# Output projection: four pairs of blocks in seven products for eight, with x loaded as it is used

## The chip, the cores and the metric

The kernel runs on all 8 cores of one Trainium2 chip. Each core computes one sequence of the batch (2048 tokens). The metric is the device time in microseconds of the slowest core. The kernel before and the kernel after are timed on the same chip.

## The reference, cut to what matters

One layer of a streaming encoder, with D = 2048 channels and 2048 tokens per sequence:

```python
h = rmsnorm(x, norm1_w) * (1.0 + sc1) + sh1
merged = sigmoid(ma) * (y_a @ w_up_a) + sigmoid(mb) * (y_b @ w_up_b)   # of h @ w_in and two recurrences
x = x + gt1 * (merged @ w_o)                    # w_o: 2048 x 2048, the output projection
h = rmsnorm(x, norm2_w) * (1.0 + sc2) + sh2
x = x + gt2 * swiglu(h, w_ffn_in, w_ffn_out)
return rmsnorm(x, final_norm_w)
```

The modulation values (sh1, sc1, gt1, sh2, sc2, gt2) come from c @ w_ada, per sequence.

## The kernel before

**Order of the work.** Tokens are taken in two stages (`s` = 0 and 1, 1024 tokens each, two halves of 512). Activations lie channel by channel: a tile `mg[k]` is 128 channels x 1024 tokens in bf16, and `H(t, hf)` is one half of it. A stage runs through the input projections and recurrences (heads), the merge, the output projection with the norm behind it, and the FFN in four quarters. Between is one long list of operations: `Graph.op` records each with the tiles it reads and writes, a cost and a key (the running sum of TensorE time `g.K` plus an offset), and `Graph.schedule` lays them out by a list scheduler from these costs. Each engine then runs its operations in the order so fixed; `emit` puts the waits in. All instructions of a kind are recorded by helpers, so they bear the helpers' lines: L478 `dense_half`, L488 `product`, L530 `plain`, L621 `norm_finish`, L799 `vgroup` (TensorE); L388 `act` (ScalarE); L392 `tt`, L412 `stt`, L495 `vtt` (VectorE); L429 every `dma`.

**Plain blocks.** A block of 128 output channels is `dense_half` for each half: 16 matmuls of 128x128 weights by 512 columns into one PSUM bank. `proj(fc, hfs, w)` does so for w_o: `stt` adds gt1 times the bank to the residual `xres[fc]` (f32), ScalarE squares the result, and VectorE adds the squares into `accD`. Blocks 0 to 9 do both halves in turn, blocks 10 to 15 first the one half of all six, then `h2half(0)` (the norm and 16 tiles of the next input), then the other half and `h2half(1)`.

**Seven for eight.** `winograd` computes a pair of output blocks as a 2 x 2 block product: the four quadrants of the weight pair (a11, a12, a21, a22, each 8 blocks of 128x128) by the even and odd input tiles and the two token halves. It takes four sums of weights on VectorE (`tt16`, 1024 columns of bf16), 7 products of 8 matmuls in place of 8, two copies out of PSUM on ScalarE, and three additions on VectorE; four results come out, two in PSUM banks and two in SBUF. The right sides (differences of the input tiles, 512 columns of bf16) are made once for all pairs by `make` in `right_sides`. It gives three new sets of 8 tiles (`t2`, `t3`, `t4`) and overwrites the second half of the even inputs by the fourth (`t1`). The merge's gates use it for blocks 2 to 15 (`w_m`), the FFN's input from its fourth block on (`w_fi`), and a variant for the FFN's output (`w_fp`). The output projection does not: it is plain throughout.

**Weights.** All weights lie in HBM as f32 and are cast by DMAs that GpSimd (POOL) issues. `wload` puts one block (1 MB read, 512 KB written) into the next of six slots of 4 KB per partition, `wload2` a pair (twice that) into the next two. A load waits until the last reader of its slots is done, and POOL issues in the order of the schedule. In stage 0 the merge also loads two w_ada chunks per block through these slots, for `ada_chunk` (one `stt` over 2048 columns with an accumulator, on VectorE). Blocks 10 and 11 of w_o have tiles of their own (`wextra`). The chunks of w_ada are worked off in stage 0: the last 14 of them 4 in the output projection (blocks 6 to 9) and 10 in the FFN's first quarter, there through one buffer at 192 KB.

**x.** The residual is loaded once more for the update: `xload(fc)` puts 512 KB into `xres[fc]` from SP. All 16 are recorded ahead of the projection; each waits for the space, which is that of the merge's right sides and `up` weights (blocks 0 to 7) and of `yT` (8 to 15), and blocks 6 and 7 in addition for `mops`, results of the merge.

Of the kernel before, what the change touches and what calls it, by code (L numbers as in the profile page):

```python
# [17 lines left out]
KB = 1024  # L18
# [225 lines left out]
def build_nc(trace=None):  # L244
    nc = bass.Bass("TRN2", target_bir_lowering=False)

    def din(name, shape):
        return nc.dram_tensor(name, list(shape), F32, kind="ExternalInput").ap()
# [13 lines left out]
    w_upb_d = din("w_upb_l", [16, 128, 1024])  # L262
    w_o_d = din("w_o_l", [16, 128, 2048])
    w_fi_d = din("w_fi_l", [44, 128, 4096])
# [4 lines left out]
    with ExitStack() as es:  # L269
# [267 lines left out]

        def right_sides(acts, t2, t3, t4):

            ev, od = acts[0::2], acts[1::2]  # L540
            hk = len(ev)
            bs = {'11': [H(t, 0) for t in ev], '21': [H(t, 0) for t in od], '22': [H(t, 1) for t in od],
                  't1': [H(t, 1) for t in ev], 't2': t2, 't3': t3, 't4': t4}

# [3 lines left out]
            def make():  # L548
                for i in range(hk):
                    sub(t3[i], bs['22'][i], bs['t1'][i])  # L550
                    sub(t2[i], t3[i], bs['11'][i], ALU.add)
                    sub(t4[i], bs['21'][i], t2[i])
                for i in range(hk):
                    sub(bs['t1'][i], bs['t1'][i], bs['11'][i])

# [415 lines left out]
        def ada_some(n, own=None):  # L971
            for _ in range(n):
                if ada_todo:
                    m = ada_todo.pop(0)
                    if own:
                        ada_chunk(m, wpair(own, w_ada_d[m - 32], psem[7]), 0.0)
                    else:
                        ada_chunk(m, wload(w_ada_d[m - 32], 2048, lag=5.0, slot=5 if nslot[0] == 5 else None), 0.0)
# [12 lines left out]
        for s in range(NST):  # L991
# [98 lines left out]

            dring[:] = [0, 1, 2, 3]
            accD = sb(HT, 1024, F32)
            rsD = sb(190 * KB, 1024, F32)
            d_q = ring(HT + 8 * KB, 3, 512, F32)
            d_t = ring(182 * KB, 4, 512, F32)

            def xload(fc):
                dma('sp', xres[fc], xT[fc, :, tok0:tok0 + ST], xsem[fc], writes=[xres[fc]], nbytes=1 << 19, key=-40,
                    after=[mops[4 + fc]] if 5 < fc < 8 else ())

            def proj(fc, hfs, w):
                def ev(hf, p):
                    x = H(xres[fc], hf)
                    stt(x, p, col(gt1h, fc), x, ALU.mult, ALU.add)
                    q = d_q() if fc else H(accD, hf)
                    act(q, x, AF.Square)
                    if fc:
                        tt(H(accD, hf), H(accD, hf), q, ALU.add)
                for hf in hfs:
                    dense_half(w, mg, hf, ev)  # L1110

            def h2half(hf):
                norm_finish(accD, rsD, hf)
                for fc in range(16):
                    t_ = d_t()
                    tt(t_, H(xres[fc], hf), H(rsD, hf), ALU.mult)
                    act(H(mg[fc], hf), t_, AF.Identity, bias=col(mod, 48 + fc), scale=col(a2, fc))
            for fc in range(16):
                xload(fc)
            for fc in range(10):  # L1120
                proj(fc, (0, 1), wload(w_o_d[fc], 2048))
                if s == 0 and 5 < fc:
                    ada_some(1)

            def wextra(i, src):
                t = sb(HT + (24 + 4 * i) * KB, 2048, BF16)
                dma('pool', t, src, psem[6 + i], writes=[t], nbytes=1 << 20, key=-20.0)
                return t
            ws = [wextra(i, w_o_d[10 + i]) for i in range(2)] + [wload(w_o_d[fc], 2048) for fc in range(12, 16)]
            for hf in range(2):  # L1130
# [112 lines left out]
            for q in range(4):  # L1243
# [8 lines left out]
                for j in range(nj):  # L1252
# [11 lines left out]
                    if s == 0 and q == 0:  # L1264
                        ada_some(2 if 0 < j < 6 else 0, sb(192 * KB, 2048, BF16))
                    if s + 1 < NST and q > 0:
# [73 lines left out]
def prep_inputs(x, c, w_ada, b_ada, norm1_w, w_in, w_gk2, b_gk2, lb_param, a_norm_w, b_norm_w,  # L1340
# [23 lines left out]
        "w_upb_l": _colchunks(f(w_up_b)[0]),  # L1364
        "w_o_l": _colchunks(f(w_o)[0]),
        "w_fi_l": _blockpairs(f(w_ffn_in)[0]),
# [41 lines left out]
```

## Time and profile before

| | us |
|---|---|
| median of 3 timed runs | 3780.18 |
| lowest, highest | 3710.52, 3817.74 |
| profiled execution, its own time | 3529.29 |
| its span on core 3, the slowest | 3528.2 |
| TensorE busy in it | 3423.4 |
| VectorE busy | 2155.5 |
| ScalarE busy | 1085.0 |

The profile is of one execution and of its slowest core, core 3. Its span runs from the first to the last instruction; its own time is 1.1 us longer. PE is TensorE, PEld its weight loads, DVE VectorE, ACT ScalarE, POOL GpSimd, SP the engine that issues the plain loads. The two output projections lie at about 882 to 1000 us (stage 0) and 2565 to 2676 us (stage 1). Times within the profile are us from its start.

### The profile page before, as it was taken

What the parts mean: (1) busy time and instruction counts of PE and PEld (TensorE: products, weight loads), DVE (VectorE), ACT (ScalarE), POOL (GpSimd) and SP (SyncE); (2) the same over time, 40 slices, a digit from 0 to 9 for tenths busy, and PEclk for the clock granted to TensorE, in tenths of its full rate; (3) what the DMA queues carried; (4) which work ended last, traced back from release to release, by engine and by line L of the source; (5) the groups of instructions that cost most, each with busy time, mean ns of one, the idle gap of its engine ahead of it and who ended that gap; (6) DMA issues with size and microseconds to landing.
All of it is one profiled execution on the core that took longest, in us unless ns stands there. A gap on an engine that the chain in (4) does not pass through costs nothing.

```text
span 3528.2 us, 48466 instructions; the slowest of 8 cores (3509.2 to 3528.2 us)
## 1 busy us (share of the span) xinstructions
PE 3423.4 (97%) x17336; PEld 1590.3 (45%) x17336; DVE 2155.5 (61%) x3769; ACT 1085.0 (31%) x1668; POOL 319.6 (9%) x564
## 2 busy tenths in 40 slices
PE   5899999999999999999999999999999999999997
PEld 2444444444444444444444444444444444444445
DVE  2277777776477866757586564544446575665747
ACT  3256445111142122121366553311114102111016
POOL 1111010111000000000010000000100000000004
PEclk8899999999999999999999999999999999999998
DMA  9966555888847575655595343354563445454552
GB/s 193 158 108 104 91 92 91 138 142 156 173 80 128 106 120 100 119 81 101 97 204 123 67 70 68 67 93 87 99 152 62 89 79 95 78 99 81 95 96 97
DMA packets 108047, 377.43 MB, mean 107 GB/s; under 512 B 11297, under 2 KB 28705, under 8 KB 92449
## 3 DMA queue, kind: packets, MB, share of 16 engines
q0 software_dynamic: 75888, 314.97, 52.9%
q1 hardware_dynamic: 31922, 59.36, 5.8%
q8 instruction: 142, 2.33, 0.3%
q14 instruction: 95, 0.78, 0.1%
HBM read 672.44 MB, written 16.78 MB: 195 GB/s over the span
## 4 chain that ended last, share of the span: by engine, by line
PE 89%; DMA 7%; DVE 2%; issue 1%; SPq 1%; ACT 0%; DVEq 0%; POOL 0%; ACTq 0%; POOLq 0%
PE PS L488 48%; PE PS L478 27%; PE PS L799 6%; PE PS L530 4%; DMA SB<-w_ada_c 1%; DMA SB<-xT 1%; DVE SB L392 1%; PE PS L682 1%; DMA SB<-w_fp_l 1%; DMA SB<-w_in_l 1%; DMA SB<-w_o_l 1%; SPq L429 1%; DMA SB<-w_m_l 1%; DMA SB<-w_fi_l 1%; PE PS L921 0%
## 5 line engine op out<-in xcount | busy, mean ns | idle before, releaser
L488 PE MATMUL PS<-SB 128*128 128x512 bf16 x8176 | 1772.4, 379 | 4.6 <-DVE SB L392 2.8
L488 PEld LDWEIGHTS PS<-SB 128*128 128x128 bf16 x8176 | 799.0, 98 | 972.9 <-issue 17.6
L478 PE MATMUL PS<-SB 128*128 128x512 bf16 (+2 forms) x5052 | 1075.9, 371 | 35.6 <-DVE SB L412 21.0
L478 PEld LDWEIGHTS PS<-SB 128*128 128x128 bf16 x5052 | 484.4, 99 | 584.8 <-issue 53.8
L388 ACT ACTIVATE SB<-SB 128x512 f32<-128x512 f32 (+5 forms) x790 | 462.9, 623 | 824.7 <-DVE SB L392 541.8
L495 DVE TENSOR_TENSOR SB<-SB 128x1024 bf16<-128x1024 bf16 (+2 forms) x1000 | 536.9, 563 | 240.3 <-PE PS L488 161.1
L392 DVE TENSOR_TENSOR SB<-PS,SB 128x512 f32<-128x512 f32 (+2 forms) x536 | 359.7, 673 | 374.1 <-PE PS L488 257.5
L388 ACT ACTIVATE SB<-PS 128x512 f32<-128x512 f32 (+2 forms) x546 | 328.7, 614 | 677.5 <-PE PS L488 371.4
L412 DVE SCALAR_TENSOR_TENSOR SB<-PS,SB 128x512 f32<-128x512 f32 (+2 forms) x528 | 365.6, 712 | 254.1 <-PE PS L478 106.1
L392 DVE TENSOR_TENSOR SB<-SB 128x512 f32<-128x512 f32 (+6 forms) x639 | 377.6, 611 | 152.3 <-ACT SB L388 120.4
L388 ACT ACTIVATE PS<-PS 128x512 f32<-128x512 f32 x158 | 92.0, 582 | 793.1 <-PE PS L488 754.8
L412 DVE SCALAR_TENSOR_TENSOR SB<-SB,PS 128x128 f32<-128x128 f32 (+3 forms) x452 | 208.8, 463 | 168.5 <-PE PS L478 135.2
L388 ACT ACT_TABLE_LOAD x158 | 202.7, 1283 | 125.1 <-PE PS L478 62.4
L799 PE MATMUL PS<-SB 128*128 128x512 bf16 x1024 | 230.1, 379 | 1.0 <-DMA SB<-w_v_l 1.0
L412 DVE SCALAR_TENSOR_TENSOR SB<-SB 128x2048 bf16<-128x2048 bf16 (+2 forms) x160 | 212.8, 1349 | 7.2 <-ACT SB L388 5.4
L799 PEld LDWEIGHTS PS<-SB 128*128 128x128 bf16 x1024 | 98.0, 98 | 114.8 <-issue 2.0
L530 PE MATMUL PS<-SB 128*128 128x512 bf16 x640 | 141.6, 379 | 0.0
L429 POOL DMA_DIRECT2D SB<-w_fi_l x88 | 46.4, 528 | 944.7 <-PE PS L488 784.1
L530 PEld LDWEIGHTS PS<-SB 128*128 128x128 bf16 x640 | 62.5, 98 | 74.1 <-issue 1.1
L429 POOL DMA_DIRECT2D SB<-w_in_l x100 | 52.9, 532 | 451.3 <-PE PS L478 210.3
L420 DVE CAST SB<-PS 128x512 bf16<-128x512 f32 x68 | 46.7, 689 | 63.2 <-PE PS L799 61.2
L429 POOL DMA_DIRECT2D SB<-w_fp_l x48 | 25.3, 528 | 473.0 <-PE PS L488 473.0
(55 smaller groups left out, 862.3 us busy)
## 6 DMA issues: line engine op xcount, KB each, us to landing
SB<-w_fi_l POOLq DMA_DIRECT2D x88, 1024.0 KB, 8.6
SB<-w_fp_l POOLq DMA_DIRECT2D x48, 768.0 KB, 6.9
SB<-w_in_l POOLq DMA_DIRECT2D x70, 512.0 KB, 6.9
SB<-xT SPq DMA_DIRECT2D x64, 512.0 KB, 22.9
SB<-w_ada_l POOLq DMA_DIRECT2D x64, 512.0 KB, 7.1
SB<-w_m_l POOLq DMA_DIRECT2D x32, 1024.0 KB, 9.0
SB<-w_ada_c POOLq DMA_DIRECT2D x32, 512.0 KB, 22.3
SB<-w_v_l POOLq DMA_DIRECT2D x32, 512.0 KB, 6.2
```

Of the source, the lines that this page charges most:

```text
L388: return g.op('act', lambda e: e.activation(out=out.ap, in_=in_.ap, func=func, **kw), reads=[in_] + aps, writes=[out], cost=cost, key=key, ...
L392: return g.op('dve', lambda e: e.tensor_tensor(out=outap if outap is not None else out.ap, in0=in0ap if in0ap is not None else in0.ap, in1 ...
L412: return g.op('dve', lambda e: e.scalar_tensor_tensor(out=out.ap, in0=in0.ap, scalar=v, in1=in1.ap, op0=op0, op1=op1, **kw), reads=[in0, i ...
L420: g.op('dve', lambda e: e.tensor_copy(out=outap if outap is not None else out.ap, in_=inap if inap is not None else in_.ap), reads=[in_], ...
L429: return g.op(q, lambda e: e.dma_start(out=oa, in_=ia), reads=list(reads), writes=list(writes), dsem=sem, nbytes=nbytes, cost=0.6, key=key ...
L478: fns = [(lambda e, k=k: e.matmul(p.ap, w.ap[:, k * 128:(k + 1) * 128], H(acts[k], hf).ap, start=(k == 0), stop=(k == nk - 1))) for k in ks]
L488: fns = [(lambda e, k=k: e.matmul(p.ap, w.ap[:, k * 128:(k + 1) * 128], acts[k].ap, start=(first and k == 0), stop=(k == nk - 1), skip_gro ...
L495: g.op('dve', lambda e: e.tensor_tensor(out=out, in0=in0, in1=in1, op=op), reads=reads, writes=writes, cost=0.16 + n * 0.00052, key=key)
L530: mm([(lambda e, k=k: e.matmul(p.ap, wk[k].ap, H(acts[k], hf).ap, start=(k == 0), stop=(k == nk - 1))) for k in range(k0, k0 + GK)], wk[k0 ...
L682: mm([lambda e, p=p, k=k, hf=hf: e.matmul(p.ap, w.ap[:, (k - k0) * 128:(k - k0 + 1) * 128], H(hT[k], hf).ap, start=(k == k0), stop=(k == k ...
L799: fns = [(lambda e, i=i, j=j, p=p, tb=tb: e.matmul(p.ap, hT[4 * i + j].ap[:, tb * 128:(tb + 1) * 128], ws[i].ap[:, j * 512:(j + 1) * 512], ...
```

## The change

Blocks 2 to 9 become four pairs through `winograd`; blocks 0, 1 and 10 to 15 stay plain. The right sides of `mg` are made in four new sets of tiles, so that `mg` itself stays as it is for the plain blocks behind (`t1` is given). They are recorded behind block 1 with a key 8 us ahead. Sets `o_1` and `o_2` lie where the last tiles of `hT` were, `o_3` and `o_4` where the merge's results were kept. The projection's PSUM ring has six banks in place of four. x is loaded for blocks 0 to 5 ahead; every further `xload` is recorded behind a block or pair and waits (`after`) for the last x update recorded before it. The extra w_o tiles move to 202 KB and to the start of `hT`. The four w_ada chunks of the projection go to the FFN's first quarter, which takes 14, alternating between two buffers.

```diff
@@ -260,7 +260,8 @@
     w_v_d = din("w_v_l", [16, 128, 2048])
     w_upa_d = din("w_upa_l", [16, 128, 1024])
     w_upb_d = din("w_upb_l", [16, 128, 1024])
-    w_o_d = din("w_o_l", [16, 128, 2048])
+    w_o_d = din("w_o_l", [8, 128, 2048])
+    w_op_d = din("w_op_l", [4, 128, 4096])
     w_fi_d = din("w_fi_l", [44, 128, 4096])
     w_fp_d = din("w_fp_l", [3, 8, 128, 3072])
     w_fo_d = din("w_fo_l", [16, 128, 1024])
@@ -535,23 +536,30 @@
         def rr(t, c):
             return t.ap.rearrange("p (n t) -> p n t", t=c)
 
-        def right_sides(acts, t2, t3, t4):
+        def right_sides(acts, t2, t3, t4, t1=None):
 
             ev, od = acts[0::2], acts[1::2]
             hk = len(ev)
             bs = {'11': [H(t, 0) for t in ev], '21': [H(t, 0) for t in od], '22': [H(t, 1) for t in od],
-                  't1': [H(t, 1) for t in ev], 't2': t2, 't3': t3, 't4': t4}
+                  't1': t1 or [H(t, 1) for t in ev], 't2': t2, 't3': t3, 't4': t4}
+            b12 = [H(t, 1) for t in ev]
 
             def sub(out, x, y, op=ALU.subtract):
                 vtt(out.ap, x.ap, y.ap, op, [x, y], [out], 512, key=-8.0)
 
             def make():
-                for i in range(hk):
-                    sub(t3[i], bs['22'][i], bs['t1'][i])
+                for i in range(hk if t1 else 0):
+                    sub(t1[i], b12[i], bs['11'][i])
+                    sub(t2[i], bs['22'][i], t1[i])
+                for i in range(hk if t1 else 0):
+                    sub(t3[i], t2[i], bs['11'][i])
+                    sub(t4[i], bs['21'][i], t2[i])
+                for i in range(0 if t1 else hk):
+                    sub(t3[i], bs['22'][i], b12[i])
                     sub(t2[i], t3[i], bs['11'][i], ALU.add)
                     sub(t4[i], bs['21'][i], t2[i])
-                for i in range(hk):
-                    sub(bs['t1'][i], bs['t1'][i], bs['11'][i])
+                for i in range(0 if t1 else hk):
+                    sub(b12[i], b12[i], bs['11'][i])
 
             def again():
                 for i in range(hk):
@@ -973,7 +981,7 @@
                 if ada_todo:
                     m = ada_todo.pop(0)
                     if own:
-                        ada_chunk(m, wpair(own, w_ada_d[m - 32], psem[7]), 0.0)
+                        ada_chunk(m, wpair(own[m % 2], w_ada_d[m - 32], psem[6 + m % 2]), 0.0)
                     else:
                         ada_chunk(m, wload(w_ada_d[m - 32], 2048, lag=5.0, slot=5 if nslot[0] == 5 else None), 0.0)
                     blk = m // 16
@@ -1088,24 +1096,47 @@
                 merge_b(fc)
 
 
-            dring[:] = [0, 1, 2, 3]
+            dring[:] = [0, 1, 2, 3, 4, 5]
+            dpos[0] = 0
+            spos[0] = 2
             accD = sb(HT, 1024, F32)
             rsD = sb(190 * KB, 1024, F32)
             d_q = ring(HT + 8 * KB, 3, 512, F32)
             d_t = ring(182 * KB, 4, 512, F32)
 
+            r_so = ring(194 * KB, 4, 1024, BF16)
+            o_tt = [sb(o_ * KB, 512, F32) for o_ in (188, 190, 192, 74)]
+            o_n = [0]
+
+            def r_to():
+                o_n[0] += 1
+                return o_tt[o_n[0] % 4]
+            o_1, o_2, o_3, o_4 = [[sb(o_ + KB * i, 512, BF16) for i in range(8)]
+                                  for o_ in (HT + 14 * KB, HT + 22 * KB, 172 * KB, 180 * KB)]
+            o_rights, o_sums, _ = right_sides(mg, o_2, o_3, o_4, o_1)
+            lastx = [None]
+
             def xload(fc):
                 dma('sp', xres[fc], xT[fc, :, tok0:tok0 + ST], xsem[fc], writes=[xres[fc]], nbytes=1 << 19, key=-40,
-                    after=[mops[4 + fc]] if 5 < fc < 8 else ())
+                    after=[lastx[0]] if lastx[0] else ())
+
+            def add_x(fc, hf, p):
+                x = H(xres[fc], hf)
+                lastx[0] = stt(x, p, col(gt1h, fc), x, ALU.mult, ALU.add)
+                q = d_q() if fc else H(accD, hf)
+                act(q, x, AF.Square)
+                if fc:
+                    tt(H(accD, hf), H(accD, hf), q, ALU.add)
+
+            def proj2(i, wp):
+                def evac(c11, c12, c21, c22):
+                    for n_, c_ in enumerate((c11, c12, c22, c21)):
+                        add_x(2 + 2 * i + n_ // 2, (0, 1, 1, 0)[n_], c_)
+                winograd(wp, 8, o_rights, r_so, r_to, evac)
 
             def proj(fc, hfs, w):
                 def ev(hf, p):
-                    x = H(xres[fc], hf)
-                    stt(x, p, col(gt1h, fc), x, ALU.mult, ALU.add)
-                    q = d_q() if fc else H(accD, hf)
-                    act(q, x, AF.Square)
-                    if fc:
-                        tt(H(accD, hf), H(accD, hf), q, ALU.add)
+                    add_x(fc, hf, p)
                 for hf in hfs:
                     dense_half(w, mg, hf, ev)
 
@@ -1115,18 +1146,22 @@
                     t_ = d_t()
                     tt(t_, H(xres[fc], hf), H(rsD, hf), ALU.mult)
                     act(H(mg[fc], hf), t_, AF.Identity, bias=col(mod, 48 + fc), scale=col(a2, fc))
-            for fc in range(16):
+            for fc in range(6):
                 xload(fc)
-            for fc in range(10):
+            for fc in range(2):
                 proj(fc, (0, 1), wload(w_o_d[fc], 2048))
-                if s == 0 and 5 < fc:
-                    ada_some(1)
+                xload(6 + fc)
+            o_sums()
+            for i in range(4):
+                proj2(i, wload2(w_op_d[i]))
+                xload(8 + 2 * i)
+                xload(9 + 2 * i)
 
             def wextra(i, src):
-                t = sb(HT + (24 + 4 * i) * KB, 2048, BF16)
+                t = sb((202 * KB, HT + 4 * KB)[i], 2048, BF16)
                 dma('pool', t, src, psem[6 + i], writes=[t], nbytes=1 << 20, key=-20.0)
                 return t
-            ws = [wextra(i, w_o_d[10 + i]) for i in range(2)] + [wload(w_o_d[fc], 2048) for fc in range(12, 16)]
+            ws = [wextra(i, w_o_d[2 + i]) for i in range(2)] + [wload(w_o_d[fc], 2048) for fc in range(4, 8)]
             for hf in range(2):
                 for i in range(6):
                     proj(10 + i, (hf,), ws[i])
@@ -1262,7 +1297,7 @@
                     elif q > 0 or j > 2:
                         hidden2(j, wload2(w_fi_d[hc]))
                     if s == 0 and q == 0:
-                        ada_some(2 if 0 < j < 6 else 0, sb(192 * KB, 2048, BF16))
+                        ada_some(2 if 0 < j < 8 else 0, [sb(188 * KB, 2048, BF16), sb(192 * KB, 2048, BF16)])
                     if s + 1 < NST and q > 0:
                         for _ in range(3 if q == 2 else 2):
                             if nexta[0] < 64:
@@ -1362,7 +1397,8 @@
         "w_v_l": w_v,
         "w_upa_l": _colchunks(f(w_up_a)[0]),
         "w_upb_l": _colchunks(f(w_up_b)[0]),
-        "w_o_l": _colchunks(f(w_o)[0]),
+        "w_o_l": _colchunks(np.concatenate([f(w_o)[0][:, :256], f(w_o)[0][:, 1280:]], axis=1)),
+        "w_op_l": _blockpairs(f(w_o)[0][:, 256:1280].reshape(2048, 4, 2, 128).transpose(0, 2, 1, 3).reshape(2048, 1024)),
         "w_fi_l": _blockpairs(f(w_ffn_in)[0]),
         "w_fp_l": np.stack([_blockpairs(w_fo[q * 1536:q * 1536 + 1536]) for q in range(3)]),
         "w_fo_l": _colchunks(w_fo_last),
```

## Rows read from the trace of the kernel before

**Rows 1.** The profile page: span and cores; busy us of each engine, share of the span.
```profile
span 3528.2 us, 48466 instructions; the slowest of 8 cores (3509.2 to 3528.2 us)
...
PE 3423.4 (97%) x17336; PEld 1590.3 (45%) x17336; DVE 2155.5 (61%) x3769; ACT 1085.0 (31%) x1668; POOL 319.6 (9%) x564
```

**Rows 2.** Windows: us; busy of PE, PEld, DVE, ACT, POOL; clock, DMA share, GB/s.
```profile
614.00:863.00 249.00, 248.15 (x1149) 112.39 (x1150) 178.09 (x269) 47.38 (x80) 34.31 (x66) 1.00 0.84 142
2561.00:2630.00 69.00, 69.00 (x321) 31.24 (x320) 28.94 (x41) 11.33 (x18) 4.22 (x8) 1.00 0.73 169
1020.00:1130.00 110.00, 110.00 (x511) 49.86 (x510) 81.56 (x133) 22.80 (x37) 9.35 (x18) 1.00 0.73 120
1130.00:1200.00 70.00, 69.81 (x324) 31.53 (x323) 53.02 (x99) 11.79 (x25) 3.76 (x8) 1.00 0.58 107
```

**Rows 3.** Waits of TensorE (total, times, longest): whole span of core 3; core 5.
```profile
PE PS L478 <- DVE SB L412: 21.0, 9, 5.0
...
PE PS L478 <- DMA SB<-w_o_l: 4.6, 1, 4.6
...
PE PS L478 <- DMA SB<-w_o_l: 5.7, 1, 5.7
```

**Rows 4.** The chain of waits around both projections: start, us, what.
```profile
872.12 28.13 DMA SB<-w_o_l
...
2554.43 102.74 PE PS L478 x476
```

**Rows 5.** The timeline at the first projection (start, us, engine), and w_ada's loads.
```profile
863.02 37.69 SPq L429 DMA_DIRECT2D SB<-xT  x16
...
871.42 24.34 PE L478 MATMUL PS<-SB 128*128 128x512 bf16 x112
...
1019.85 0.53 POOL L429 DMA_DIRECT2D SB<-w_ada_l  x1 [18.42 <-DVE SB L495]
...
1131.02 0.53 POOL L429 DMA_DIRECT2D SB<-w_ada_l  x1 [2.56 <-DVE SB L412]
```

**Rows 6.** Windows of TensorE behind the stall: us, PE busy, clock, DMA share.
```profile
900.00:904.00 4.00, 3.61 (x9) 0.50 1.02 235
904.00:908.00 4.00, 4.00 (x14) 0.72 1.01 252
```

**Rows 7.** Groups by shape, 882 to 980 and 2425 to 2554: busy, mean ns.
```profile
L412 DVE SCALAR_TENSOR_TENSOR SB<-PS,SB 128x512 f32<-128x512 f32 x26 | 19.5, 750 | 39.1 <-PE PS L478 39.1
L392 DVE TENSOR_TENSOR SB<-SB 128x512 f32<-128x512 f32 x23 | 15.9, 691 | 13.9 <-ACT SB L388 13.9
L412 DVE SCALAR_TENSOR_TENSOR SB<-SB 128x2048 bf16<-128x2048 bf16 x4 | 9.1, 2284 | 0.0
...
L495 DVE TENSOR_TENSOR SB<-SB 128x1024 bf16<-128x1024 bf16 x22 | 15.1, 687 | 12.3 <-PE PS L488 11.8
L388 ACT ACTIVATE SB<-PS 128x512 f32<-128x512 f32 x20 | 11.9, 597 | 15.7 <-PE PS L488 15.7
```

**Rows 8.** The timeline of VectorE behind the first projection: the FFN's right sides.
```profile
1009.03 8.74 DVE L392 TENSOR_TENSOR SB<-SB 128x512 f32<-128x512 f32 x14
...
1019.23 3.44 DVE L495 TENSOR_TENSOR SB<-SB 128x512 bf16<-128x512 bf16 x10
...
1029.76 2.09 DVE L495 TENSOR_TENSOR SB<-SB 128x512 bf16<-128x512 bf16 x6
```

**Rows 9.** DMA queues, packets, MB and share, 863 to 900.3.
```profile
q0 software_dynamic: 1032, 3.60, 58.7%
q1 hardware_dynamic: 1089, 4.00, 41.9%
```

**Rows 10.** Landing times: all w_fi loads; the one issued at 1029.51; all xT.
```profile
SB<-w_fi_l POOLq DMA_DIRECT2D x88, 1024.0 KB, 8.6
...
SB<-w_fi_l POOLq DMA_DIRECT2D x1, 1024.0 KB, 8.3
...
DMA to landing us min/median/max: 2.2/7.5/42.2
```

## Prediction before the result

> **What bounds the kernel now.** I read the busy shares and the cores' spans first, then windows by stage, then the chain of waits, and last the transfers around the one stall found. TensorE is busy 97% of the span [rows 1]: whoever adds nothing to TensorE and takes no wait from it changes nothing. The cores lie within 0.6% of each other (3509.2 to 3528.2 us) [rows 1], so core 3, the slowest, stands for all. The kernel passes the output projection twice, once in each half of the tokens. Around the second pass TensorE is never idle (69 us busy of 69 in the stretch read), while VectorE is busy 42% of it [rows 2]. Around the first pass it is idle once: a wait of 4.6 us for w_o on core 3, and of 5.7 us on core 5, where it is longest [rows 3]. Other waits of TensorE lie outside the projection.
>
> The stall's story is in the chain and the timeline [rows 4, 5]. The weights of block 2 take the first half of the slot pair that w_m of block 15 held, whose last quarter (a22) is read by the last product; so that load is issued at 872.12, as the last of the loads that the end of the merge sets free, and lands 28.13 us later. SP has meanwhile put all 16 loads of x into the same 16 DMA engines, from 863.02 on. Blocks 0 and 1 run 112 matmuls with the merge's tail, until 895.76; the weights come at 900.25. Behind the wait the granted clock is 0.50 for 4 us and 0.72 for the next 4, so the engine first runs at 1.2 GHz, then at 2.4 again [rows 6]: (1 - 0.50) x 3.6 busy us + (1 - 0.72) x 4 = 2.9 us more. The stall costs 4.6 + 2.9 = 7.5 us.
>
> **Part 1, products.** In each pass blocks 2 to 9 take 8 x 2 x 16 = 256 matmuls now and 4 x 7 x 8 = 224 afterwards; 64 fewer in both passes. In the long chain piece 476 matmuls take 102.74 us, 0.216 each [rows 4], so 64 x 0.216 = 13.8 us. Nothing hides TensorE, so all of it is gained if nobody makes it wait.
>
> **Part 2, what VectorE gets per pair.** Four left-side sums over 1024 columns, three f32 additions, four updates of x and four additions of squares. By their durations [rows 7]: 4 x 0.69 + 3 x 0.69 + 4 x 0.75 + 4 x 0.69 = 10.6 us, within 56 x 0.216 = 12.1 us of TensorE. That is an upper bound, since back to back they overlap: 14 f32 additions take 8.74 us, 0.62 each [rows 8], which makes about 9.6 us, 80%. In the first pass's merge VectorE is busy 72% and in the FFN output stage 76%, while TensorE misses 0.85 us of 249 and 0.2 of 70 [rows 2]. ScalarE has two copies and four squares per pair, 0.60 each, under 4 us [rows 7]. I take 0.5 us in all for small waits, the merge's share of 0.85 in 249 on the pairs' 97 us and a little more. The bounds are 0 (TensorE has no wait there that could go) and 5 us, the longest wait for an x update's or merge's stt in the whole trace [rows 3], once.
>
> **Part 3, the right sides.** 32 bf16 differences of 512 columns come to stand between the last read of hT and the first pair. Ten such take 3.44 us [rows 8], so 32 take 11.0 us. In the second pass hT is free at 2554.4, 48 matmuls of the merge and 64 of blocks 0 and 1 follow, 24.2 us; the product with t3 comes 4 products (6.9 us) later, the one with t4 6 products (10.4 us): the last group is due at +34.6 us. By then VectorE owes ten operations of the merge (6.9), the sums (11.0), blocks 0 and 1 (4 x 0.75 + 2 x 0.69 = 4.4), the left sides of two pairs (5.5) and two additions (1.4): 29.2 of 34.6 us. t1 and t2 come first in the order and are due at +25.9 to +27.7: 6.9 + 5.5 + 2.8 + 4.4 = 19.6. It fits, and costs 0. The upper bound goes by a sum twice as wide at its full duration, 0.69 [rows 7]: 22 us in place of 11, 40.3 of 34.6, 5.7 us late in each pass. Below 0 nothing is to be had, as TensorE has no wait there.
>
> **Part 4, loads.** In the first pass the pair's 1 MB load (w_op 0) takes both halves of w_m 15's slots, so it also cannot be issued before 872.12, behind w_op 1 and the two extra w_o tiles: six half-MB units in total, as now. What falls away is x: only blocks 0 to 5 are loaded ahead. Up to 900.3 the weights' queue moved 3.60 MB, the x queue 4.00 MB in 41.9% of 37.3 us [rows 9], 3.9 us per MB; six x loads are 3.15 MB, 0.85 MB fewer, 3.3 us earlier: w_op 0 lands at about 897.0. The first product is due at 895.76, so I forecast a wait of 1.2 us, and a second of some 0.8 for the first left side behind it: 2 us, too short to expect the slow clock. Of the 7.5 us, 5.5 come back. Bounds: all 7.5 if the queue drains quicker; nothing if the 1 MB load, twice as long as what it replaces, lands at 900.25 again. In the second pass no such conflict exists: that slot pair is free a whole merge block earlier, as no w_ada load takes slots there.
>
> The paced x loads come when the last update before them is done: blocks 8 and 9 behind the first pair, needed 36 us later; blocks 14 and 15 behind the fourth, needed by block 14 after 5 x 3.45 = 17 us. One x load lands after 7.5 us in the median, counting the bursts [rows 10]. SP has nothing behind them but later x loads and stores. So no cost.
>
> Four w_ada chunks per kernel go from the first projection to the FFN's first quarter, which takes 14 instead of 10, with two buffers. One costs 2.28 us of VectorE and a small addition, 2.4 [rows 7]. Today's ten are issued from 1019.85 to 1131.02 [rows 5], so nine at most run in the stretch 1020 to 1130, where VectorE is busy 81.6 of 110 us [rows 2]; five more make 93.6 of 110. I take 0, with 0 to 2.4 us, one chunk in the way once, as bounds. The w_fi load of the second block is freed earlier, which helps nobody, as TensorE waits for none of them now.
>
> **One rule weighed.** The case most against part 3 is that the sums hold up the very loads they run beside. In the trace a w_fi load issued at 1029.51, with six bf16 sums right behind it, landed after 8.3 us, and the median of all w_fi loads is 8.6 [rows 8, 10]: no delay. The Trainium skill, page "SBUF — State Buffer", section "SBUF: two separate sides", says that GpSimd and VectorE share a port pair under an exclusive lock, and that DMAs issued from GpSimd wait with their descriptors while VectorE runs a two-port operation. By that rule the sum would be that of rival (d) below, by the rows it stays at 19; the trace does not bear the rule out for these sums.
>
> **Sum.** 13.8 + 5.5 - 0.5 = 18.8 us, say 19. The profiled execution took 3529.3 us (span 3528.2), so it would take 3510.3, a ratio of 0.9946. The timed runs lie higher, median 3780.18, from 3710.52 to 3817.74, 7% above it; I take the ratio to carry over: 3780.18 x 0.9946 = 3760 us. These runs spread by 2.8%, five times the effect; about 2% is what a measurement of this kernel can tell from no change.
>
> **Rivals.**
> (a) *The load stays late.* The stall moves from block 2 to the first pair and is as long as now, since the transfer is twice as large and pairs need their left sides before product 2. For it: the weights' queue and the x queue together fill the DMA engines there (58.7 + 41.9% [rows 9]), and only 0.85 MB falls away. Then 13.8 - 0.5 = 13.3 us are gained, or 7 if it is 4 us longer and the slow clock lasts 2 us more: 3766 to 3773 us.
> (b) *Slower: VectorE becomes the bound of the pairs.* Place: a product into bank b may not start before `tt(u, b, t)` has read it, with one product (1.73 us) of slack, and that addition stands behind four x updates and squares of the pair before. Price: if each pair waits 3 us, 8 x 3 = 24 us, and 6 us of slow clock (two times the 2.9 above). It decides from 19 / 8 = 2.4 us per pair, that is VectorE at 14.5 us a pair. Against it: 10.6 at most. 3529.3 - 19 + 30 = 3540, times 3780.18 / 3529.3 is 3792 us.
> (c) *The right sides come too late* in both passes, by up to 6 us each with a dip of the clock: 13.8 + 5.5 - 12 - 5 = 2 us gained, 3778 us. Against it: 5 us of slack.
> (d) *Port.* Sums of 11 us block the descriptors of w_op 0: it lands near 907, a stall of 11 + 2.9 us in place of 2: 19 - 12 = 7 us gained, 3773 us.
> (e) *The change does not do what it says*: the products are not fewer. The code's count is against it; 3780 us.
>
> **Chances.** Forecast 0.62, (a) 0.20, (b) 0.05, (c) 0.08, (d) 0.03, (e) 0.02. All of them but (b) lie between 3760 and 3780, so the width of the range is that of the runs: the lowest of before, less the largest gain (13.8 + 7.5 = 21.3 us, 23 at the pace of the timed runs), is about 3687; the highest is 3797 at the forecast's ratio and 3829 with (b). I take 3687 to 3815. No case reaches 2% by itself; a forecast at -0.5% with this spread can come out beyond -2% in 8 of 100, and beyond +2% in 3, half of it (b). So faster 0.08, within 2% 0.89, slower 0.03.
>
> **What would show it.** 64 fewer TensorE instructions (17272). Second projection: TensorE still without idle time, the stretch from merge to FFN 6.9 us shorter. First pass: the wait on w_o gone, one on w_op of 0 to 2 us, granted clock above 0.9 throughout. VectorE near 80% in the pairs. Wrong would be: waits of TensorE on VectorE's lines in the pairs (b, c), a w_op wait over 4 us with clock 0.5 behind it (a), a w_op load issued near 870 that takes over 30 us (d), or waits on x at the fourth pair or block 14.

## The result, and the profile after

| | before | after |
|---|---|---|
| profiled execution, its own time, us | 3529.29 | 3505.16 |
| its span on the slowest core | 3528.2 | 3504.1 |
| median of 8 timed runs | 3568.9 | 3508.78 |
| ratio after to before | | 0.9937 [0.9922, 0.9952] |

By the ratio the changed kernel is faster by 0.63%, 22 us of 3529 (17 to 28). Forecast was 0.9946, 19 us. The absolute forecast, 3760 us with a range of 3687 to 3815, missed by far: it was scaled from three runs of 3710 to 3818 us, where five later runs of the same kernel took 3527 to 3588. The ratio leaves out runs like that of the changed kernel at 3714.84 us, in which the cores of one die had a clock of 0.93 while those of the other were done after 3494 to 3505 us.

The page of the changed kernel (span, then busy time and instructions):

```profile
span 3504.1 us, 48197 instructions; the slowest of 8 cores (3490.7 to 3504.1 us)
PE 3388.6 (97%) x16942; PEld 1585.1 (45%) x17272; DVE 2207.8 (63%) x3889; ACT 1094.1 (31%) x1684; POOL 315.2 (9%) x556
```

The count of matmuls is to be read from the weight loads, PEld: 17272, 64 fewer than 17336 [rows 1]; this trace lacks 330 records of PE itself. The lines have moved by one: L479 is `dense_half`, L489 `product`, L531 `plain`.

**The length of a projection.** Cores start the stage at different times, and their spans differ within one run, by 19 us before and 13 us after, so I compare a stretch instead: from the issue of the last w_upb load to the first matmul of the FFN. On core 3 of before and core 6 of after (timeline: start, us, what):

```profile
859.17 0.53 POOL L429 DMA_DIRECT2D SB<-w_upb_l  x1 [5.85 <-PE PS L478]
1000.20 4.05 PE L530 MATMUL PS<-SB 128*128 128x512 bf16 x18
...
2542.88 0.53 POOL L429 DMA_DIRECT2D SB<-w_upb_l  x1 [6.38 <-PE PS L478]
2676.23 4.05 PE L530 MATMUL PS<-SB 128*128 128x512 bf16 x18
```

```profile
859.45 0.53 POOL L430 DMA_DIRECT2D SB<-w_upb_l  x1 [5.85 <-PE PS L479]
986.22 4.05 PE L531 MATMUL PS<-SB 128*128 128x512 bf16 x18
...
2527.02 0.53 POOL L430 DMA_DIRECT2D SB<-w_upb_l  x1 [6.38 <-PE PS L479]
2653.46 2.75 PE L531 MATMUL PS<-SB 128*128 128x512 bf16 x12
```

Before: 141.0 and 133.35 us. After: 126.8 and 126.4. Over all cores the median of the first pass goes from 141.1 (138.9 to 142.0) to 127.6 (126.4 to 130.8), 13.5 us; the second from 133.3 to 126.4 on every core, 6.9 us. Together 20.4 us, nearly all of the gain. The second pass shows what 126.4 means: TensorE without a wait. So the first pass lost 141.1 - 133.3 = 7.8 us to its stall before, and loses 1.2 after. The other 2 us of the 22 are not located; the interval of the ratio is wider than that.

What is left of the stall is a wait for the first pair's weights, 0 to 2.5 us by core (0, 1.5, 0, 1.7, 0.5, 1.8, 0.2, 2.5 on cores 0 to 7). On core 7, and in the timeline of cores 6 and 3:

```profile
PE PS L489 <- DMA SB<-w_op_l: 2.5, 1, 2.5
```

```profile
863.30 82.48 SPq L430 DMA_DIRECT2D SB<-xT  x16
...
869.76 0.53 POOL L430 DMA_DIRECT2D SB<-w_op_l  x1 [0.29 <-issue]
...
873.26 0.53 POOL L430 DMA_DIRECT2D SB<-w_op_l  x1 [2.98 <-PE PS L489]
...
895.00 1.03 PE L489 MATMUL PS<-SB 128*128 128x512 bf16 x4
...
896.21 47.64 PE L489 MATMUL PS<-SB 128*128 128x512 bf16 x216 [0.18 <-DMA SB<-w_op_l]
...
883.18 22.18 PE L489 MATMUL PS<-SB 128*128 128x512 bf16 x102 [1.69 <-DMA SB<-w_op_l]
```

The reader is to see three things: the 16 x loads now spread over 82.48 us instead of 37.69 [rows 5]; the load at 873.26 lands after 22.81 us (the chain of waits has it), where core 3 took 28.13 before [rows 4]; and TensorE goes on at 896.21 on core 6. The four matmuls at 895.00 belong to the second pair, whose weights were there; the schedule puts them ahead of the first pair's. Before, four of block 3 stood in that place.

On core 7 the wait of 2.47 us is followed by a low clock, which costs 1.8 us more (its first pass takes 130.75 us; windows of TensorE: us, busy, clock, DMA share, GB/s):

```profile
884.00:888.00 4.00, 1.64 (x5) 0.81 1.02 243
888.00:892.00 4.00, 4.00 (x16) 0.76 1.01 217
```

**How much of x is out of the way.** From 4 us behind the last w_upb issue until the late load had landed, core 6 moved this, first before (36.71 us), then after (32.62 us):

```profile
q0 software_dynamic: 1100, 3.73, 63.2%
q1 hardware_dynamic: 1010, 3.72, 38.2%
...
q0 software_dynamic: 614, 3.20, 57.2%
q1 hardware_dynamic: 997, 3.64, 38.9%
```

q0 has the weights, q1 has x. In the mean of the eight cores x fell from 3.88 to 3.59 MB, by 0.3 and not by 0.85: on core 6 a seventh load of x has been issued by then, as block 0's updates are done.

VectorE in the four pairs of the second pass (core 7; us, then busy of PE, PEld, DVE, ACT, POOL, clock, DMA share, GB/s):

```profile
2554.00:2602.00 48.00, 48.00 (x224) 21.72 (x222) 35.27 (x54) 14.31 (x24) 3.53 (x7) 1.00 0.76 172
```

It is busy 35.27 of 48 us, 73%, and TensorE misses nothing.

### The profile page after: what moved, and what is told of

The parts are those of the page before. It is cut to its first block, busy times and chain, and to the rows that moved or that the text cites. A ratio compares the mean times of both kernels' runs of the same rounds, so it can differ in the third digit from the quotient of the medians.

```text
span 3504.1 us, 48197 instructions; the slowest of 8 cores (3490.7 to 3504.1 us)
## 1 busy us (share of the span) xinstructions
PE 3388.6 (97%) x16942; PEld 1585.1 (45%) x17272; DVE 2207.8 (63%) x3889; ACT 1094.1 (31%) x1684; POOL 315.2 (9%) x556
## 4 chain that ended last, share of the span: by engine, by line
PE 89%; DMA 6%; DVE 2%; issue 2%; ACT 0%; SPq 0%; DVEq 0%; POOL 0%; ACTq 0%; POOLq 0%
PE PS L489 51%; PE PS L479 24%; PE PS L807 6%; PE PS L531 4%; DMA SB<-w_ada_c 1%; DMA SB<-xT 1%; DVE SB L393 1%; PE PS L690 1%; DMA SB<-w_in_l 1%; DMA SB<-w_m_l 1%; DMA SB<-w_op_l 1%; DMA SB<-w_fi_l 1%; DMA SB<-w_fp_l 0%; DVE SB L413 0%; PE PS L929 0%
## 5 line engine op out<-in xcount | busy, mean ns | idle before, releaser
L489 PE MATMUL PS<-SB 128*128 128x512 bf16 x8454 | 1860.0, 379 | 13.6 <-DVE SB L393 1.9
L489 PEld LDWEIGHTS PS<-SB 128*128 128x128 bf16 x8624 | 843.0, 98 | 1025.2 <-issue 16.6
L479 PE MATMUL PS<-SB 128*128 128x512 bf16 (+2 forms) x4438 | 955.4, 370 | 34.8 <-DVE SB L413 16.3
L496 DVE TENSOR_TENSOR SB<-SB 128x512 bf16<-128x512 bf16 (+2 forms) x1096 | 581.3, 557 | 236.8 <-PE PS L489 163.4
L479 PEld LDWEIGHTS PS<-SB 128*128 128x128 bf16 x4540 | 434.8, 99 | 514.9 <-issue 44.2
L393 DVE TENSOR_TENSOR SB<-PS,SB 128x512 f32<-128x512 f32 (+2 forms) x560 | 376.1, 674 | 385.1 <-PE PS L489 266.5
L413 DVE SCALAR_TENSOR_TENSOR SB<-PS,SB 128x512 f32<-128x512 f32 (+3 forms) x512 | 352.7, 710 | 194.3 <-PE PS L489 71.5
L413 DVE SCALAR_TENSOR_TENSOR SB<-SB 128x2048 bf16<-128x2048 bf16 (+2 forms) x176 | 224.3, 1293 | 7.2 <-ACT SB L389 5.1
L807 PE MATMUL PS<-SB 128*128 128x512 bf16 x997 | 227.0, 379 | 1.6 <-issue 0.3
L531 PE MATMUL PS<-SB 128*128 128x512 bf16 x625 | 140.1, 379 | 0.8
L531 PEld LDWEIGHTS PS<-SB 128*128 128x128 bf16 x640 | 62.4, 98 | 74.1 <-issue 1.1
```

What stands on the lines that cost most here:

```text
L393: return g.op('dve', lambda e: e.tensor_tensor(out=outap if outap is not None else out.ap, in0=in0ap if in0ap is not None else in0.ap, in1 ...
L413: return g.op('dve', lambda e: e.scalar_tensor_tensor(out=out.ap, in0=in0.ap, scalar=v, in1=in1.ap, op0=op0, op1=op1, **kw), reads=[in0, i ...
L479: fns = [(lambda e, k=k: e.matmul(p.ap, w.ap[:, k * 128:(k + 1) * 128], H(acts[k], hf).ap, start=(k == 0), stop=(k == nk - 1))) for k in ks]
L489: fns = [(lambda e, k=k: e.matmul(p.ap, w.ap[:, k * 128:(k + 1) * 128], acts[k].ap, start=(first and k == 0), stop=(k == nk - 1), skip_gro ...
L496: g.op('dve', lambda e: e.tensor_tensor(out=out, in0=in0, in1=in1, op=op), reads=reads, writes=writes, cost=0.16 + n * 0.00052, key=key)
L531: mm([(lambda e, k=k: e.matmul(p.ap, wk[k].ap, H(acts[k], hf).ap, start=(k == 0), stop=(k == nk - 1))) for k in range(k0, k0 + GK)], wk[k0 ...
```

## The experiments

The columns of the two passes are the stretch above, the median over the cores. The rows of e1 to e4 and e10 are over cores 0 to 3 alone (e2's trace stands for e10); on these cores the changed kernel has 127.3 and 126.4. The ratio is to the kernel before, run on the same chip.

| run | first pass | second pass | ratio |
|---|---|---|---|
| before | 141.1 | 133.3 | 1 |
| changed | 127.6 | 126.4 | 0.9937 [0.9922, 0.9952] |
| e9, changed again | 127.4 | 126.4 | 0.9939 [0.9922, 0.9957] |
| e1, x all ahead (cores 0 to 3) | 131.6 | 126.4 | 0.9961 [0.9946, 0.9976] |
| e2 / e10, plain and paced (cores 0 to 3) | 137.6 | 133.3 | 0.999 [0.998, 1.0] |
| e3, sums twice (cores 0 to 3) | 130.9 | 127.9 | 0.9966 [0.9952, 0.9981] |
| e4, extras late (cores 0 to 3) | 126.7 | 126.4 | 0.9956 [0.994, 0.9973] |
| e5, five pairs | 130.2 | 126.6 | 0.9952 [0.9937, 0.9966] |
| e6, five pairs, extras late | 130.5 | 126.8 | 0.9966 [0.9953, 0.9979] |
| e7, six pairs | 129.7 | 125.1 | 0.9946 [0.9929, 0.9963] |
| e8, 12 more additions per pair | 127.9 | 126.2 | 0.9959 [0.9944, 0.9973] |
| e11, 16 more, first in order | 133.2 | 130.5 | 0.9986 [0.9965, 1.0008] |
| e12, w_ada back | 129.3 | 126.4 | 0.9949 [0.9931, 0.9967] |

The reason for cores 0 to 3: e1, e3 and e4 ran on one chip, and there the second pass of cores 4 to 7 is 0.9 to 2.9 us longer in e1 and 1.8 to 2.0 in e4, without a wait. The granted clock shows it (e4, core 4, window of TensorE):

```profile
2580.00:2590.00 10.00, 10.00 (x46) 0.94 0.99 185
```

What lowers it there is not known. Cores 0 to 3 of e1 and e4 have the 126.4 us of the changed kernel.

### e1: all x loads ahead

```diff
-            for fc in range(6):
+            for fc in range(16):
                 xload(fc)
...
-                xload(6 + fc)
...
-                xload(8 + 2 * i)
-                xload(9 + 2 * i)
```

The condition on the last update is replaced by the old one on `mops`.

> The changed kernel with all 16 loads of x recorded ahead of the projection, as before the change. Theory (the x burst delays the weights, and pacing brings the first pass's stall back): the load of the first pair is again the last of six half-MB units beside 4.0 MB of x and lands near 900, so TensorE waits 4 to 6 us on w_op in the first pass and has the slow clock behind it, and only the products (13.8 us) are gained: ratio to the kernel before about 0.996. Rival (the pacing is worth nothing, the order of the weights decides): wait of 0 to 2.5 us as with the change, ratio 0.9937.

The ratio is the one expected, 0.9961, about 8 us above the changed kernel, of which the stretches show 4; and the wait is 1.7 to 3.2 us, not 4 to 6. The first pass is 131.6, 5.2 us over a pass without a wait (against 7.8 before and 1.2 with the change). Core 0: wait, and clock behind it (windows of TensorE: us, busy, clock, DMA share, GB/s):

```profile
884.70 1.03 PE L489 MATMUL PS<-SB 128*128 128x512 bf16 x4
888.38 11.89 PE L489 MATMUL PS<-SB 128*128 128x512 bf16 x46 [2.65 <-DMA SB<-w_op_l]
```

```profile
888.00:892.00 4.00, 3.62 (x10) 0.57 1.07 259
```

A wait of 2.65 us is followed by a clock of 0.57 over 3.62 busy us, 1.6 us more. A wait of 1.69 us on core 3 of the changed kernel is not followed by one:

```profile
884.00:888.00 4.00, 4.00 (x20) 1.00 0.94 188
```

So the rival falls: without pacing the stall is 4 us longer. And the theory is short of a cause, since 2.6 of the 7.8 us went without any pacing. Counted from the last w_upb issue, TensorE stops at 36.6 us in before, e1 and e2 alike (37.5 on cores 4 and 5 of e1), but the late load lands after 41.4 us before and 39.1 in e1 (medians of the cores). The transfers show what goes with it. In the 32 us from 4 us behind the last w_upb issue (mean of 8 cores), the weights' queue moved 3.02 MB before and 3.14 in e1, with 854 packets against 603; the x queue 3.33 MB against 3.07, with about as many bytes per packet as before. The weights in loads of twice the size went in larger packets and had the larger share. A second difference goes with it: the next load of weights is issued 36.3 us behind w_upb in e1, 29.4 before, so less of it is in the queue beside the late one. No run separates the two, such as plain blocks with 1 MB loads.

### e2 and e10: plain blocks, x paced

```diff
-            for fc in range(16):
+            for fc in range(6):
                 xload(fc)
             for fc in range(10):
                 proj(fc, (0, 1), wload(w_o_d[fc], 2048))
+                xload(6 + fc)
```

with the new condition, `after=[lastx[0]]`.

> The kernel before with the x loads paced by its updates (6 ahead, each further one behind a block) and all blocks plain. Theory: the wait of 4.6 us on w_o in the first pass and the 2.9 us of slow clock go, nothing else changes: 6 to 7.5 us, ratio 0.998. Rival (pacing helps only together with the pairs, or costs a wait on x): ratio 1.000 or above, with a wait of TensorE or VectorE on x.

> The kernel of e2 (plain blocks, x paced) once more, for a time. e2's trace shows the wait on w_o at 2.3 to 3.1 us in place of 4.6 and the first projection at 137.7 us in place of 141.1. Theory: 3 to 4 us less than before, ratio 0.999. Rival (my first reckoning): 6 to 7.5 us, 0.998.

Waits on w_o of 2.3 to 3.1 us in place of 4.0 to 5.5 on the same cores, the first pass 137.6 in place of 141.1, ratio 0.999 [0.998, 1.0]. The late load lands 39.1 us behind w_upb, as in e1. Pacing by itself is worth 3.5 us of the stall, and in time just about what can be told from nothing. e2 itself gave no ratio, e10 did. Neither the 6 to 7.5 us of my first reckoning nor the rival of no gain in the stretch holds.

### e3: the right sides computed twice

```diff
-                for i in range(hk if t1 else 0):
+                for i in list(range(hk if t1 else 0)) * 2:
```

(in both loops of `make`)

> The changed kernel with each of the 32 right-side differences computed twice (same values), 11 us more of VectorE ahead of the first pair in each pass. Theory (VectorE has about 5.4 us of slack there): 5 to 6 us late in each pass, waits of TensorE on VectorE in the first pair of 5 us each, with or without slow clock: 10 to 15 us slower than the changed kernel, ratio to before 0.9965 to 0.998. Rival (the slack is larger than reckoned, as the sums run in gaps between the merge's operations): no wait, ratio 0.9937 to 0.994.

The ratio, 0.9966, is in the expected range, the place is not. On cores 0 to 3 the second pass is 1.5 us longer, not 5 to 6, and the first 3.6; of the 10 us that the ratio gives, the stretches hold 5. The slack behind the merge is larger than I reckoned, as the changed kernel's core 7 shows (VectorE timeline, the first, last and one of the merge's operations):

```profile
2518.32 1.43 DVE L496 TENSOR_TENSOR SB<-SB 128x512 bf16<-128x512 bf16 x4 [0.24 <-PE PS L489]
...
2540.17 0.68 DVE L393 TENSOR_TENSOR SB<-SB 128x512 bf16<-128x512 f32 x1
...
2544.96 3.10 DVE L496 TENSOR_TENSOR SB<-SB 128x512 bf16<-128x512 bf16 x9
```

The sums begin at 2518.3, while the merge's last seven products (the last readers of hT) run until 2528.4, and slip a few at a time between the merge's operations; the last ends at 2548.06, and the pairs' first product starts at 2552.58. My count had the last one due at the seventh product, 10.4 us later, with 5.4 us to spare; it was done 4.5 us ahead of the first. With 11 us more in front, updates of blocks 0 and 1 and left sides come late instead. That is argued and not shown: the waits found are small ones on several things: 0.9 us on a copy, the rest put down to w_op, 1.6 to 3.8 us by core in the first pass and 0 to 2.0 in the second.

### e4: the extra w_o loads later

```diff
+            x1 = [lastx[0]]
...
-                dma('pool', t, src, psem[6 + i], writes=[t], nbytes=1 << 20, key=-20.0)
+                dma('pool', t, src, psem[6 + i], writes=[t], nbytes=1 << 20, key=-20.0, after=x1)
```

> The changed kernel with the two extra w_o loads (blocks 10 and 11) held until block 1 has updated x, so that 1 MB less stands ahead of the first pair's weights. Theory (the weights' queue sets the rest of the wait): the wait on w_op in the first pass, 0 to 2.5 us on the eight cores now, goes to 0 on all, ratio 0.9930 to 0.9937. Rival (the release of the slots at 873 sets it, not the queue): the waits stay.

The first pair's load lands after 17.3 us on core 3 (13.5 to 18.2 over the cores) in place of 22 to 25, and the wait on w_op is gone on all cores:

```profile
SB<-w_op_l POOLq DMA_DIRECT2D x1, 1024.0 KB, 17.3
```

The first pass is only 0.6 us shorter on cores 0 to 3 (126.7 against 127.3), as half of all cores now wait 0.3 to 1.3 us on a ScalarE copy of that pair. The theory of the queue holds; as a version it brings nothing that can be measured (0.9956, overlapping the changed kernel's interval, and not below it).

### e5, e6 and e7: five and six pairs

```diff
-            for fc in range(2):
-                proj(fc, (0, 1), wload(w_o_d[fc], 2048))
-                xload(6 + fc)
             o_sums()
-            for i in range(4):
+            for i in range(5):
```

with w_o laid out to match; e6 adds e4's edit; e7 has `range(6)` and a tail of four blocks.

> Blocks 0 to 9 as five pairs, no plain block ahead of them; blocks 10 to 15 as with the change. 16 matmuls fewer per pass, 6.9 us in both. The right sides now have no two plain blocks in front; the first pair starts when the merge ends and needs t2 3.5 us, t3 6.9 us, t4 10.4 us later. Theory (the sums run in the gaps of the merge's tail; in the changed kernel the last was done 8 us after the merge's end): waits of 0 to 2 us per pass, ratio to before 0.992 (0.9937 less 0.0020 for the products). Rival (my reckoning before, where the sums start only when hT is free and need 11 us behind the merge's operations): 4 to 6 us late per pass with a dip of the clock, ratio 0.994 to 0.996.

> As e5 with the two extra w_o loads held until the first pair has updated x. Theory: the second pair's weights (the ones behind the queue now) come before they are needed, first pass without a wait on w_op: 0 to 2.5 us less than e5, ratio 0.991 to 0.992. Rival (e5's waits are on VectorE alone): same as e5.

> As e6 with blocks 0 to 11 as six pairs and only four blocks in the tail whose second half covers the norm of the first. Another 6.9 us of products go. Theory (ScalarE's 16 activations of the norm end 0.7 us before the FFN starts in the changed kernel, 6.9 us of cover are taken away in each pass): TensorE waits on ScalarE 3 to 6 us at the start of the FFN in each pass, so nothing is gained on e6 or 1 to 5 us are lost: ratio 0.991 to 0.9935. Rival (the plain products read the tiles in order and run just behind ScalarE): wait under 2 us, ratio 0.9895 to 0.990.

All three expectations count the products wrong: a pair takes 56 matmuls for 64, so one more pair saves 8 matmuls per pass (1.7 us) and not 16. Against that, e5 loses this (core 0, first and second pass):

```profile
PE PS L489 <- DVE SB L413: 3.6, 1, 3.6
...
PE PS L489 <- DVE SB L413: 1.6, 2, 1.3
```

The second pass is 126.6, as long as with four pairs. In the first the 3.6 us stand where VectorE, without a break, makes the last merge results and the right sides between them, and the first pair wants the results; it is 2.5 us longer than in the changed kernel. e6 is no better (waits on w_op of 1.7 to 4.8 us in the first pass, and on VectorE on half the cores). In e7 the tail of four blocks costs nothing: the second pass is 125.1, 1.5 to 1.8 less than e5 and e6, with 1.6 us or a little more on VectorE and no wait on ScalarE in it. The rival of e7 holds there. So what covers the right sides is the two plain blocks ahead of the pairs; the blocks behind them are not needed for the norm in that number. A version with blocks 2 to 11 in pairs, which keeps the cover in front, was not tried. None of the three beats the changed kernel.

### e8 and e11: more work for VectorE in the pairs

```diff
                         add_x(2 + 2 * i + n_ // 2, (0, 1, 1, 0)[n_], c_)
+                        for _ in range(3):
+                            tt(d_x, xres[0].cols(0, 256), xres[0].cols(256, 512), ALU.add)
```

e11 has 4 in place of 3 and `key=-6.0`. Results are not used.

> The changed kernel with 12 more VectorE additions of 256 f32 columns per pair (0.3 to 0.4 us each, results unused), about 4 to 4.9 us per pair. VectorE is busy 35.3 us of 48 in the four pairs now, 8.8 of 12.1 per pair; it would be 13 to 13.7. Theory (TensorE waits only when VectorE's sum passes 12.1 us per pair): 1 to 1.6 us late per pair, less the slack at the start, 3 to 12 us over both passes: ratio 0.9945 to 0.997. Rival (b) of the prediction (the places of the additions between two products of one bank matter before the sum does): waits in every pair of 2 us or more, 16 us or more, ratio 0.998 or above.

> The changed kernel with 16 more VectorE additions of 256 f32 columns per pair (results unused), put ahead of the pair's other work in the order. At 0.35 us back to back they make 8.9 + 5.6 = 14.5 us per pair, the point of rival (b). Theory (TensorE waits once the sum passes 12.1): 2.4 us per pair less a slack of some 6 us at the start of each pass: 7 to 12 us over both passes with the clock's dips, ratio 0.9955 to 0.998. Rival (additions spill behind the pairs as in e8): no wait, ratio as e9.

e8, core 1, the pairs of the first pass:

```profile
896.00:944.00 48.00, 48.00 (x224) 21.67 (x223) 44.44 (x83) 13.21 (x22) 3.16 (x6) 1.00 0.75 157
```

VectorE is busy 93%, and TensorE works 48.00 of 48 us. Nobody waits for the added operations themselves, and they may slip behind those that TensorE needs. Part of the additions went behind the pairs, so this tests 11.1 us a pair, not 13. e11 does not let them go: the passes are 5.8 and 4.1 us longer than in e9, with waits like these on core 2:

```profile
PE PS L479 <- DVE SB L393: 4.3, 2, 3.0
...
PE PS L479 <- DVE SB L393: 3.4, 2, 2.1
```

They stand at L479, the plain blocks behind the pairs, where the backlog shows, and 0.4 us at the pairs themselves. 9.9 us in both passes for 5.6 us a pair more: in the expected 7 to 12 us, by the expected cause, though at another place. The ratio, 0.9986, lies above the expected 0.9955 to 0.998 with an interval that reaches into it, and would be 17 us over e9; the stretches hold 9.9. Rival (b)'s mechanism, waits in every pair, shows in neither.

### e12: the four w_ada chunks back

```diff
                 proj2(i, wload2(w_op_d[i]))
+                if s == 0 and i % 2:
+                    ada_some(2)
...
-                        ada_some(2 if 0 < j < 8 else 0, ...
+                        ada_some(2 if 0 < j < 6 else 0, ...
```

> The changed kernel with the four w_ada chunks back in the first projection, two behind the second pair and two behind the fourth, through the slot ring, and 10 in the FFN's first quarter. Theory: the chunks cost nothing in the FFN, but here they take a slot pair and so shorten the distance of the weights' loads from two pairs to one: a wait of 0 to 3 us on w_op for the pair behind, ratio as e9 plus 0 to 0.001. Rival (moving them made the FFN's first quarter slower, and this brings it back): 2 to 5 us faster than e9.

The first pass is 1.9 us longer than in e9, with the wait on w_op spread over up to three places (1.5 to 3.6 us in all by core) and one of 0.2 to 0.6 us on w_fi on seven cores. From the end of the first projection to the last w_upb load of the second pass it takes 1542.9 us in the median of the cores against 1541.7 in e9, where the cores of one run scatter by 5 us. So moving the chunks costs nothing that shows, and saves the slots.

### e9: the changed kernel again

> The changed kernel itself once more, on the chip of the runs beside it. Theory: ratio 0.9937 again, within 0.0015. Rival (the ratio differs between chips by as much as the effects looked for; e8 ran its two projections as fast as the changed kernel and was timed at 0.9959): ratio 0.995 to 0.996.

0.9939 [0.9922, 0.9957] on another chip. The rival falls. Ratios of single experiments scatter by about 0.002 all the same: e8 has the changed kernel's passes to 0.3 us, e4 on cores 0 to 3 to 0.6, and both have other ratios. I read differences of 0.1% from the stretches, not from the times.

## Why the prediction was right or wrong

**The ratio was right** (0.9946 forecast, 0.9937 [0.9922, 0.9952] and 0.9939 measured), and the second pass to the tenth: 6.9 us.

**The absolute time was wrong.** The step that failed is in the sum: "I take the ratio to carry over: 3780.18 x 0.9946 = 3760 us". The ratio did; the 3780.18 was the wrong number to scale. It was 5 to 7% above each of the five later runs of the same kernel (3527 to 3588). The low end of the range was wrong in the same way, as it was put at "the lowest of before, less the largest gain". The record already held a profiled execution at 3529.3, 5 to 8% below the three runs, and the sum worked out from it, 3510.3, is 1.5 us from the measured 3508.78. A range over both would have had to begin below 3510.

**Part 1, products:** 64 fewer (PEld), 13.8 us. Right; shown by the second pass.

**Part 2, VectorE per pair:** forecast 80%, measured 73%, no wait. e8 at 93% still has none. Right in sign, 0.8 us per pair too dear (9.6 against 35.27 / 4 = 8.8). The 0.5 us set aside for small waits did not come either: the second pass has none.

**Part 3, right sides:** no wait, as forecast; the working was wrong. "In the second pass hT is free at 2554.4" and the sums begin there: on core 7 they began 10 us ahead of that point, a few at a time, because each sum needs only its own piece of that space. The slack is larger than the 5.4 us I gave: 11 us more cost 1.5 in the second pass (e3). It is the plain blocks in front that give it (e5).

**Part 4, loads:** forecast that of 7.5 us 5.5 come back. Measured 7.8 and 6.6. The size is about right, the working is not, and that they agree is in part luck. I gave it all to "0.85 MB fewer" of x, landing the load 3.3 us earlier; only 0.3 MB fewer were moved until it landed, 1.1 us at the same 3.9 us per MB, and it landed 3.9 us earlier (41.4 and 37.5 us behind w_upb, medians). Pacing alone brings 3.5 us (e2), the larger weight loads and what comes with them 2.6 (e1), both 6.6. In e1 the wait is back at 2.65 us with a dip of the clock on core 0: rival (a)'s stall, 5.2 of the 7.8 us. "Too short to expect the slow clock" held for 1.69 us on core 3, with a clock of 1.00 behind it, and failed on core 7: 2.47 us and clocks of 0.81 and 0.76 in the two windows of 4 us, where "above 0.9 throughout" was the sign of being right.

**The w_ada chunks:** VectorE was to be busy 93.6 of 110 us in the FFN's first quarter. Core 6, the stretch of 110 us from 1005:

```profile
1005.00:1115.00 110.00, 109.47 (x502) 49.83 (x510) 92.08 (x153) 23.47 (x40) 12.14 (x23) 1.00 0.84 146
```

92.08; PE's 502 records beside PEld's 510 show that the half us missing from its 110 is a gap in the records. Right.

**Rivals.** (b), (c) and (e) did not happen. (d), the port: w_op loads with bf16 sums running beside them landed sooner than before, 22.81 us (core 6) against 28.13 (core 3). No sign of it, as the row of before had it. The rule weighed speaks of two-port operations, and no row here shows that these sums are such.

## What to carry to other kernels

Compare the same stage between two marks of the program, on all cores, before comparing times: here two profiles of the changed kernel agree within 0.3 us, where ratios scatter by 0.002, 7 us. Look at the cores one by one, and at their clock, before taking a median. When a transfer is late, look at everything in the DMA engines at that moment and at the size of each load; issuing the competing loads later and making the late loads larger both helped, by 3.5 and 2.6 us. If the timed runs and the profiled execution differ by several per cent, let the range hold both.

## What the runs showed of the hardware that I had not expected

- Between 2.0 and 2.5 us the length of TensorE's wait did not decide whether a slow clock followed. Behind 2.01 us (e9, core 7) the clock was 0.50 in a window of 2 us, behind 2.21 us (e9, core 0) 1.00:

```profile
882.25 49.33 PE L489 MATMUL PS<-SB 128*128 128x512 bf16 x220 [2.01 <-DMA SB<-w_op_l]
883.67:885.67 2.00, 2.00 (x6) 0.50 0.94 215
...
883.48 26.71 PE L489 MATMUL PS<-SB 128*128 128x512 bf16 x123 [2.21 <-DMA SB<-w_op_l]
884.69:886.69 2.00, 2.00 (x11) 1.00 1.12 223
```

  Behind 2.47 us (core 7 of the changed kernel) it was low, behind 2.48 us (e8, core 0) 1.00. At 0.50 the engine is at 1.2 GHz, at 1.00 at 2.4.
- With two queues in the same 16 DMA engines, the larger share went together with larger packets (e1 differs from before in more than that): 3.02 MB in 854 packets before, 3.14 MB in 603 packets in e1, while x, its own packets unchanged, fell from 3.33 to 3.07 MB in the same 32 us.
- VectorE was busy 93% of 48 us in which TensorE depends on it in every product group, without TensorE waiting once (e8, core 1); about a fifth of that work, 44.44 - 35.27 us, nobody waits for (35.27 is the changed kernel's, core 7).
